# Weight layout of three out projections, place of the q blocks, and the last down projection's last chunk by token halves, in a three-layer block kernel on one core

## The chip, the cores and the metric

The kernel is one program for one core of a Trainium2 chip. The metric is device time in microseconds (us). Engines: TensorE (PE; PEld is its weight load), VectorE (DVE), ScalarE (ACT), GpSimd (POOL) and SyncE (SP), which issues most DMAs. Each engine runs its own instructions in program order and waits on semaphores for the others.

## The reference, cut to what matters

512 tokens of 1024 channels pass through three layers, all in float32; the third layer's output is normalised.

```python
# layer 1: gated delta rule                  # layer 2: stick-breaking attention
h = h + gdn_mixer(rms_norm(h), ...)          # ends in o @ gdn_w_out      (1024 x 1024)
h = h + swiglu(rms_norm(h), w_gu, w_down)    # 1024 -> 2 x 2816 -> 1024
h = h + sb_mixer(rms_norm(h), k, v, w_q)     # q = rms_norm(hn @ w_q) per head; ends in o @ sb_w_out
h = h + swiglu(rms_norm(h), w_gu, w_down)
# layer 3: latent attention and window attention, gated and added
x = h + mixed @ w_out_2                      # 1024 x 1024
x = x + conv_ffn(rms_norm(x), w_up, conv_w, conv_b, w_down)
out = rms_norm_2(x, final_norm_g)
```

In the stick-breaking mixer each head has scores z, softplus(z), a sum of it over later keys, weights exp(...) and values.

## The kernel before, in words

Everything is kept transposed: 128 channels on the partitions, 512 tokens along the free axis. `hT` holds the residual in 8 chunks (c), `ps` is the PSUM with 8 banks of 512. A product keeps float32 precision with three matmuls (`three`, L1745 to L1749): weights high times input high, weights high times input low, weights low times input high. The inputs' high and low parts are `xh` and `xl`, in 8 chunks (kc). One *block* is such a triple for one 128 x 128 piece of weights.

All weights come as one stream of units of 16 blocks (1 MB) in the order of use. SP loads unit u into `raw` (slot u % 2) once unit u-2 is split. ScalarE makes the high part `wh` (`split_hi`, L343, instruction L351), and VectorE then the low part `wl` (`split_lo`, instruction L933). Both wait for the count `units_used`, that is until TensorE has done unit u-2, for `wh` and `wl` have two slots too. TensorE waits for both parts (`unit_ready`). `hi_half` (L509) and `lo_half` (L1160) do the same in two instructions of 1024 columns.

An out projection (gdn_out, sb_out, mix_out) has 4 units. Output chunks 0 to 3 are accumulated in banks 0 to 3 input chunk by input chunk, since the mixer delivers input chunks one at a time; chunks 4 to 7 follow one after the other. In the stream the weights lie by output chunk: unit 0 has c 0 and 1, unit 1 has c 2 and 3, unit 2 c 4 and 5, unit 3 c 6 and 7 (`out_block`, L1840). Some blocks of c 0 to 3 are placed between other work of the mixers (`early_out` L2058, `OUT_AT`; steps 5 to 8 of the second mixer; steps 12 to 15 of the third and after them). `out_rest` (L1846) does what is left: kc 6 and 7 (7 in gdn_out) for c 0 to 3, then c 4 to 7. VectorE adds each finished chunk to `hT` and splits units 2 and 3 on the way (`split_out`, L974).

In the first mixer's last head, VectorE multiplies the normed values with their gain (`scale_out`, L1199, instruction L1201) and with silu(z) (`om_gdn`, L1291); ScalarE's copy (L384) and VectorE's `out_low` (L1206) then make input chunk 7.

The second mixer runs in steps t = 0 to 9 (TensorE's loop L2254 to L2280, ScalarE's `step` L731, VectorE's `step` L1371). On TensorE a step has the values of head t-2 (`head_values`, L2247), the scores of head t (L2209), the sum of squares of q of head t+1 (`q_sums`, L2196), the mask (L2219), the sums over later keys of head t-1 (`rest`, L2232 to L2236), and then filler: the dense block row of q of head t+3 (`q_dense`, 8 blocks, t = 0 to 4), or blocks of sb_out (3, 1, 1 and 19 in t = 5 to 8). On ScalarE a step has the square of q (`q_squares`, L690), the copy of the head's output (`head_out`, L729), copies of it into `xh` (L384), a unit's split, Ln and Exp for q's norm (L696, L698), Abs, Exp and Ln of softplus (L707, L709, L711), the Exp of head t-1's weights (L723) and softplus's high part (L717). On VectorE: `q_in` (L1341), a unit's split, `q_scale` (L1349), `remainder` (L1369), and softplus's three instructions (L1355, L1359, L1361), of which the last is its low part.

The end: the last feed-forward's down projection does 8 output chunks of 22 blocks. For the last, VectorE adds it to `hT` (L1045), ScalarE squares it (L918), TensorE adds that to the sum of squares over channels (`sum_norm_last`, L1765; fp32, two records for one matmul), ScalarE makes rstd by a table load, Ln and Exp (`make_rstd`, L367: L355, L371, L373), VectorE multiplies 8 chunks with gain and rstd (L1593), and SP sends each chunk out.

## Time and profile before

| | us |
|---|---|
| time, median of 3 runs | 2275.66 (2273.36 to 2275.94) |
| the profiled execution's own time | 2275.48 |
| its span, first to last instruction | 2273.4 |
| TensorE, matmuls | 2217.7 (98%) |
| VectorE, ScalarE, GpSimd busy | 1115.1, 923.8, 288.6 |

The span is that of one profiled execution; 2.1 us of its time lie outside it. The page gives busy time and groups of instructions; the waits name who released an engine; the windows give busy time and the granted clock of a stretch (1.00 is 2.4 GHz, 0.50 is 1.2 GHz); the timeline gives single instructions. Matmuls are pipelined: a record of 0.39 us starts 0.23 us after the one before it.

### The profile page before, as it was taken

Reading aid. Unit: us, or ns where it says so; the run is one execution under the profiler, and the core shown is the slowest. Engines: PE = TensorE matmul, PEld = TensorE weight load, DVE = VectorE, ACT = ScalarE, POOL = GpSimd, SP = SyncE. Lnnn points to the kernel's source line nnn. Section 1 sums busy time; section 2 is a strip of 40 time slices with the busy share of each in tenths; the row PEclk is TensorE's granted clock in tenths of the full one; section 3 lists DMA queues with packets and bytes.
Section 4 is the critical chain, followed back from the end, with each engine's and each line's share of the span. In section 5 each row is a group of like instructions: output and inputs, shape, how many; then the busy total and the mean of one; then the engine's idle time right before and its main releaser. Section 6 shows DMA issues by size and latency. Waiting matters only on the chain.

```text
span 2273.4 us, 28231 instructions
## 1 busy us (share of the span) xinstructions
PE 2217.7 (98%) x10980; PEld 1810.6 (80%) x10980; DVE 1115.1 (49%) x1413; ACT 923.8 (41%) x1243; POOL 288.6 (13%) x247
## 2 busy tenths in 40 slices
PE   7999999899999999998999999999999999999998
PEld 4788888688888888876888888888788777888886
DVE  5566656354443233464444432355665655555522
ACT  4544555232322234574332222255565554444311
POOL 0111112210000110001300001200000034222211
PEclk9999999999999999999999999999999999999999
DMA  3311111122222222210322222331111223222321
GB/s 134 112 56 38 47 47 38 56 93 92 92 93 105 98 86 82 77 37 17 111 92 92 96 107 93 120 109 68 67 54 56 70 69 117 92 92 94 107 95 56
DMA packets 30604, 185.37 MB, mean 82 GB/s; under 512 B 3104, under 2 KB 5536, under 8 KB 10160
## 3 DMA queue, kind: packets, MB, share of 16 engines
q1 hardware_dynamic: 28496, 176.46, 22.0%
q0 software_dynamic: 2016, 7.60, 1.0%
q8 instruction: 67, 1.10, 0.2%
q14 instruction: 25, 0.20, 0.0%
HBM read 179.83 MB, written 7.37 MB: 82 GB/s over the span
## 4 chain that ended last, share of the span: by engine, by line
PE 93%; DVE 3%; ACT 2%; issue 1%; DMA 0%; SPq 0%; POOL 0%; DVEq 0%; ACTq 0%; POOLq 0%
PE ps L1747 25%; PE ps L1749 25%; PE ps L1748 25%; PE ps L1955 4%; PE ps L2429 1%; PE ps L2372 1%; PE ps L2412 1%; PE ps L2247 1%; PE ps L2209 1%; PE ps L2439 1%; PE ps L1976 1%; DVE wl L933 0%; PE ps L1912 0%; PE ps L2370 0%; PE ps L2009 0%
## 5 line engine op out<-in xcount | busy, mean ns | idle before, releaser
L1747 PE MATMUL ps<-xh,wh 128*128 128x512 f32 x1888 | 766.1, 406 | 13.4 <-DVE wl L933 10.0
L1749 PE MATMUL ps<-xh,wl 128*128 128x512 f32 x1888 | 738.8, 391 | 0.0
L1748 PE MATMUL ps<-xl,wh 128*128 128x512 f32 x1888 | 737.4, 391 | 0.0
L351 ACT ACTIVATE wh<-raw 128x2048 fp32r<-128x2048 f32 x144 | 275.3, 1914 | 542.2 <-PE ps L1749 541.9
L933 DVE TENSOR_TENSOR wl<-raw,wh 128x2048 fp32r<-128x2048 f32 x144 | 336.6, 2337 | 310.0 <-ACT wh L351 310.0
L1747 PEld LDWEIGHTS ps<-xh,wh 128*128 128x128 f32 x1888 | 356.2, 189 | 93.3 <-issue 14.1
L1749 PEld LDWEIGHTS ps<-xh,wl 128*128 128x128 f32 x1888 | 355.4, 188 | 76.9
L1748 PEld LDWEIGHTS ps<-xl,wh 128*128 128x128 f32 x1888 | 356.6, 189 | 71.0 <-issue 4.8
L1747 PE MATMUL ps<-hid_h,wh 128*128 128x512 f32 x528 | 208.0, 394 | 0.0
L1749 PE MATMUL ps<-hid_h,wl 128*128 128x512 f32 x528 | 207.0, 392 | 0.0
L1748 PE MATMUL ps<-hid_l,wh 128*128 128x512 f32 x528 | 204.9, 388 | 0.0
L1011 DVE TENSOR_TENSOR scaled<-ps,rstd 128x1024 f32<-128x1024 f32 x44 | 53.9, 1225 | 192.9 <-PE ps L1749 192.9
L1749 PEld LDWEIGHTS ps<-hid_h,wl 128*128 128x128 f32 x528 | 99.1, 188 | 23.2
L1748 PEld LDWEIGHTS ps<-hid_l,wh 128*128 128x128 f32 x528 | 99.1, 188 | 22.2
L1747 PEld LDWEIGHTS ps<-hid_h,wh 128*128 128x128 f32 x528 | 99.3, 188 | 19.7
L1611 POOL TENSOR_TENSOR sq<-hT 128x512 f32<-128x512 f32 x41 | 48.2, 1177 | 289.9 <-DVE hT L1045 257.7
L1606 POOL TENSOR_TENSOR ssq<-hT 128x512 f32<-128x512 f32 x6 | 6.2, 1040 | 562.9 <-DVE hT L1045 507.0
L424 ACT ACTIVATE hid_h<-gu 128x512 f32 (+1 forms) x44 | 27.8, 632 | 110.2 <-DVE gu L1021 110.2
L1011 DVE TENSOR_TENSOR gu<-ps,rstd 128x1024 f32<-128x1024 f32 x22 | 26.9, 1225 | 85.8 <-PE ps L1749 85.8
L1613 POOL TENSOR_TENSOR ssq<-ssq,sq 128x512 f32<-128x512 f32 x41 | 61.4, 1498 | 3.2
L831 ACT ACTIVATE prob<-ps,nmax 128x512 f32<-128x512 f32 x32 | 22.0, 687 | 89.5 <-DVE nmax L1498 89.3
L1088 DVE SCALAR_TENSOR_TENSOR convd<-ps,vec,convd 128x511 f32<-128x511 f32 (+2 forms) x72 | 53.8, 747 | 2.0
(357 smaller groups left out, 2841.4 us busy)
## 6 DMA issues: line engine op xcount, KB each, us to landing
raw<-in_stream SPq DMA_DIRECT2D x159, 1024.0 KB, 4.8
hankd<-tabd SPq DMA_DIRECT2D x1, 3072.0 KB, 16.8
hank<-hankd POOLq DMA_DIRECT2D x4, 768.0 KB, 4.9
hT<-in_xT SPq DMA_DIRECT2D x4, 512.0 KB, 5.5
keepd<-hT POOLq DMA_DIRECT2D x1, 2048.0 KB, 9.9
hT<-keepd POOLq DMA_DIRECT2D x8, 256.0 KB, 4.6
out<-hT SPq DMA_DIRECT2D x8, 256.0 KB, 2.2
raw<-in_stream SPq DMA_DIRECT2D x2, 512.0 KB, 8.1
```

The source lines that it names most:

```text
L351: act.activation(wh[:, s, :], raw[:, s, :], ACT.Copy).then_inc(hi_made, 1)
L424: act.activation(hid_h[:, 2 * it + j, :], prod, ACT.Copy).then_inc(hid_hi_made, 1)
L933: dve.tensor_tensor(wl[:, s, :], raw[:, s, :], wh[:, s, :].bitcast(F32), ALU.subtract).then_inc(lo_made, 1)
L1011: dve.tensor_tensor(to[:, :, :], ps[:, b:b + 2, :], rstd[:, :].unsqueeze(1).to_broadcast([P, 2, SEQ]), ALU.mult).then_inc(gu_made, 1)
L1088: dve.scalar_tensor_tensor(convd[:, i, d:SEQ], ps[:, b, 0:SEQ - d], w, convd[:, i, d:SEQ], ALU.mult, ALU.add).then_inc(conv_step, 1)
L1611: pool.tensor_tensor(sq[:, :], hT[:, c, :], hT[:, c, :], ALU.mult).then_inc(squared, 1)
L1613: pool.tensor_tensor(ssq[:, :], ssq[:, :], sq[:, :], ALU.add).then_inc(summed, 1)
L1747: pe.matmul(out, w_hi, a_hi, start=start, stop=False)
L1748: pe.matmul(out, w_hi, a_lo, start=False, stop=False)
L1749: return pe.matmul(out, w_lo, a_hi, start=False, stop=stop)
L1955: m = pe.matmul(ps[:, b, cs(c)], left[:, c, :], right[:, c, :], start=True, stop=True)
L1976: m = pe.transpose(ps[:, (4, 4, 6)[k], cs(c)], T[:, c, :], mat("ident"))
```

## The change

- Stream layout (`by_half_then_chunk`): in the three out projections unit 0 has input chunks 0 to 3 of c 0 to 3, and unit 1 has chunks 4 to 7 of them. Units 2 and 3 are as before. `units_used` is counted at block (3,3) for unit 0; `half_done` counts c 0, 1, 2, 4 and 6.
- Unit 2 of each is split earlier: in gdn_out by halves among the last head's state work, in sb_out between steps 8 and 9 on ScalarE and before the low part of chunk 7 on VectorE, in mix_out before `fill_mixed(7)` on ScalarE and after the low part of chunk 7 on VectorE.
- Second mixer: the q blocks go by `Q_DENSE_AT` (head 4 by halves in steps 1 and 2, heads 5, 6, 7 in steps 3, 4, 5), `q_in` and `q_squares` by `Q_IN_AT`; the sb_out blocks are 4, 2 and 18 in steps 6 to 8; the splits of the units follow.
- Last down chunk: two passes over the 22 blocks with 256 tokens each, in banks 5 and 3; add, square, sum, Ln and Exp by halves; the gain is multiplied in by ScalarE ahead of it, rstd by VectorE over 4 chunks x 256 tokens; 8 output DMAs of 2 chunks x 256 tokens.

```diff
-HALF = {"gdn_out": 0, "sb_out": 4, "mix_out": 8}
+HALF = {"gdn_out": 0, "sb_out": 5, "mix_out": 10}
+Q_IN_AT = {2: 0, 3: 1, 4: 3, 5: 4, 6: 5, 7: 6}
+Q_DENSE_AT = {0: (3, 0, 8), 1: (4, 0, 4), 2: (4, 4, 8), 3: (5, 0, 8), 4: (6, 0, 8), 5: (7, 0, 8)}
...
-            for c in range(KC):
-                sp.wait_ge(final_made, c + 1)
-                sp.dma_start(io["out"][c * P:(c + 1) * P, :], hT[:, c, :]).then_inc(out_written, 16)
+            for k in range(8):
+                cs, tok = slice(2 * (k % 4), 2 * (k % 4) + 2), slice(256 * (k // 4), 256 * (k // 4) + 256)
+                sp.wait_ge(final_made, k // 2 + 1)
+                sp.dma_start(out_t[:, cs, tok], hT[:, cs, tok]).then_inc(out_written, 16)
...
             for c in range(TT):
                 values_out(HEADS - 1, c, 4)
+                if c >= 2:
+                    hi_half(U0["gdn_out"] + 2, c - 2)
             out_squares(HEADS - 1, 5)
...
             def step(t):
-                if t == 5:
-                    act.wait_ge(units_used, LAST_READER["sb_out"])
-                    for c in range(3):
-                        fill_chunk(om_sb, c, om_sb_made, 0)
-                q_squares(t + 2)
-                head_out(t - 2)
-                if t >= 5:
+                for h in Q_IN_AT:
+                    if Q_IN_AT[h] == t:
+                        q_squares(h)
+                head_out(t - 2)
+                if t == 6:
+                    act.wait_ge(units_used, LAST_READER["sb_out"])
+                    for c in range(4):
+                        fill_chunk(om_sb, c, om_sb_made, 0)
+                if t >= 6:
                     fill_chunk(om_sb, t - 2, om_sb_made, 0)
-                if t % 2 and t <= 5:
-                    split_hi(u0 + 2 + (t + 1) // 2)
+                if t in (1, 4, 6):
+                    split_hi(u0 + 3 + (1, 4, 6).index(t))
                 q_rstds(t + 1)
                 softplus(t)
                 weights(t - 1)
...
             for t in range(HEADS + 2):
+                if t == HEADS + 1:
+                    split_hi(U0["sb_out"] + 2)
                 step(t)
...
             fill_mixed(6)
+            split_hi(U0["mix_out"] + 2)
             fill_mixed(7)
...
-            act.activation(sq[:, :], hT[:, KC - 1, :], ACT.Square).then_inc(last_squared, 1)
-            make_rstd(6)
+            for c in range(KC - 1):
+                act.wait_ge(summed, 8 * (STATS["final"] - 1) + c + 1)
+                act.activation(hT[:, c, :], hT[:, c, :], ACT.Copy, scale=v("final_norm", c)).then_inc(gained, 1)
+            for a in range(2):
+                tok = slice(256 * a, 256 * a + 256)
+                act.wait_ge(resid_added, 8 * RESID["ffn2"] + KC + a)
+                act.activation(sq[:, tok], hT[:, KC - 1, tok], ACT.Square).then_inc(last_squared, 1)
...
+                act.activation(hT[:, KC - 1, tok], hT[:, KC - 1, tok], ACT.Copy, scale=v("final_norm", KC - 1)).then_inc(gained, 1)
+                act.wait_ge(norm_sum, 7 + a)
+                act.activation(sq[:, tok], ps[:, 6 + a, tok], ACT.Ln, bias=v("eps"), scale=1.0 / D_MODEL).then_inc(ln_made, 1)
...
+                act.activation(rstd[:, tok], sq[:, tok], ACT.Exp, scale=-0.5).then_inc(rstd_made, 1)
...
-                    if c in (3, 4, 6):
-                        split_lo(u0 + 2 + (3, 4, 6).index(c))
+                    if c in (4, 6):
+                        split_lo(u0 + 3 + (4, 6).index(c))
...
+            def finish():
+                for a in range(2):
+                    tok = slice(256 * a, 256 * a + 256)
+                    dve.wait_ge(*((chunk_done, 22) if a == 0 else (units_used, N_UNITS)))
+                    dve.tensor_tensor(hT[:, KC - 1, tok], hT[:, KC - 1, tok], ps[:, 5 - 2 * a, tok], ALU.add).then_inc(resid_added, 1)
+                    dve.wait_ge(rstd_made, 7 + a)
+                    dve.wait_ge(gained, KC + a)
+                    for q in range(2):
+                        h4 = hT[:, 4 * q:4 * q + 4, tok]
+                        dve.tensor_tensor(h4, h4, rstd[:, tok].unsqueeze(1).to_broadcast([P, 4, 256]), ALU.mult).then_inc(final_made, 1)
...
             for c in range(TT - 1):
                 state(HEADS - 1, c, 4)
+            lo_half(U0["gdn_out"] + 2, 0)
             scale_out(HEADS - 1, 5)
+            lo_half(U0["gdn_out"] + 2, 1)
             dve.wait_ge(o_scaled, HEADS)
...
             def step(t):
-                q_in(t + 2)
-                if t % 2 and t <= 5:
-                    split_lo(u0 + 2 + (t + 1) // 2)
+                for h in Q_IN_AT:
+                    if Q_IN_AT[h] == t:
+                        q_in(h)
+                if t in (1, 4):
+                    split_lo(u0 + 3 + (1, 4).index(t))
                 q_scale(t + 1)
+                if t == 6:
+                    split_lo(u0 + 5)
                 remainder(t - 1)
                 softplus(t)
...
             for c in (6, 7):
+                if c == 7:
+                    split_lo(U0["sb_out"] + 2)
...
+            split_lo(U0["mix_out"] + 2)
             split_out("mix_out", "ffn2", "norm2_2")
...
-            dve.wait_ge(rstd_made, 7)
-            for c in range(KC):
-                dve.scalar_tensor_tensor(hT[:, c, :], hT[:, c, :], v("final_norm", c), rstd[:, :], ALU.mult, ALU.mult).then_inc(final_made, 1)
...
+            def last_chunk(a):
+                tok = slice(256 * a, 256 * a + 256)
...
+                for fc in range(FC):
...
+                    m = three(ps[:, 5 - 2 * a, tok], wh[:, s, w], wl[:, s, w], hid_h[:, fc, tok], hid_l[:, fc, tok], fc == 0, fc == FC - 1)
...
+                    if a and fc == 6:
+                        sum_norm_last(0)
...
-                u, b = U0[name] + c // 2, KC * (c % 2) + kc
+                u, b = (U0[name] + kc // 4, 4 * (kc % 4) + c) if c < 4 else (U0[name] + c // 2, KC * (c % 2) + kc)
...
+                if (c, kc) == (3, 3):
+                    m.then_inc(units_used, 1)
...
-                q_dense(t + 3)
-                if t == 5:
+                if t in Q_DENSE_AT:
+                    q_dense(*Q_DENSE_AT[t])
+                if t == 6:
                     unit_ready(U0["sb_out"])
                     pe.wait_ge(q_copied, HEADS)
-                    for kc in range(3):
+                    for kc in range(4):
                         x_chunk_ready("sb_out", kc)
                         out_block("sb_out", 0, kc)
-                elif t == 6:
-                    x_chunk_ready("sb_out", 3)
-                    out_block("sb_out", 0, 3)
                 elif t == 7:
-                    x_chunk_ready("sb_out", 4)
-                    out_block("sb_out", 0, 4)
+                    unit_ready(U0["sb_out"] + 1)
+                    for kc in (4, 5):
+                        x_chunk_ready("sb_out", kc)
+                        out_block("sb_out", 0, kc)
...
-            sum_norm_last(6)
+            last_chunk(0)
+            last_chunk(1)
+            sum_norm_last(1)
```

## Rows read from the trace of the kernel before

**Rows 1.** The page: busy engines, and the two splits of a unit.

```profile
PE 2217.7 (98%) x10980; PEld 1810.6 (80%) x10980; DVE 1115.1 (49%) x1413; ACT 923.8 (41%) x1243; POOL 288.6 (13%) x247
...
L351 ACT ACTIVATE wh<-raw 128x2048 fp32r<-128x2048 f32 x144 | 275.3, 1914 | 542.2 <-PE ps L1749 541.9
L933 DVE TENSOR_TENSOR wl<-raw,wh 128x2048 fp32r<-128x2048 f32 x144 | 336.6, 2337 | 310.0 <-ACT wh L351 310.0
```

**Rows 2.** TensorE's waits, whole span: who released it, us in total, times, longest.

```profile
PE ps L1747 <- DVE wl L933: 10.0, 3, 3.4
PE ps L2247 <- ACT la L723: 5.8, 3, 2.5
```

**Rows 3.** Windows: length, busy time (count) of each engine, PEclk, DMA share, GB/s.

```profile
446.40:449.80 3.40, 3.40 (x10) 2.63 (x9) 1.91 (x1) 0.00 (x0) 3.32 (x2) 0.50 0.97 311
1036.90:1054.00 17.10, 14.96 (x59) 10.76 (x60) 8.89 (x7) 10.05 (x10) 1.28 (x1) 0.80 0.01 1
...
1878.10:1881.50 3.40, 3.40 (x15) 2.80 (x16) 3.10 (x2) 0.00 (x0) 3.26 (x2) 1.00 0.66 226
```

**Rows 4.** Timeline, gdn_out and mix_out: start, us, instruction, count, [idle before <-releaser].

```profile
432.67 0.60 ACT L543 ACTIVATE on<-ps 128x512 f32<-128x512 f32 x1 [0.87 <-PE ps L2029]
...
438.04 0.69 DVE L1206 TENSOR_TENSOR xl<-om_gdn,xh 128x512 fp32r<-128x512 f32 x1 [0.70 <-ACT xh L384]
...
438.88 0.47 PE L1747 MATMUL ps<-xh,wh 128*128 128x512 f32 x1 [1.67 <-DVE xl L1206]
...
1869.51 0.69 DVE L1586 TENSOR_TENSOR xl<-hT,xh 128x512 fp32r<-128x512 f32 x1 [1.92 <-ACT xh L864]
...
1878.05 0.47 PE L1747 MATMUL ps<-xh,wh 128*128 128x512 f32 x1 [3.38 <-DVE wl L933]
```

**Rows 5.** Timeline, second mixer: steps 4 and 5, and the start of step 8.

```profile
998.91 2.32 PE L2247 MATMUL ps<-la,v_tok 128*128 128x512 f32 x8
...
1001.27 0.60 ACT L729 ACTIVATE om_sb<-ps 128x512 f32<-128x512 f32 x1
...
1005.77 1.22 ACT L707 ACTIVATE soft<-ps 128x1280 f32<-128x1280 f32 x1
...
1007.37 0.44 PE L1747 MATMUL ps<-xh,wh 128*128 128x512 f32 x1
1007.57 1.49 DVE L1369 TENSOR_TENSOR la<-la,ps 128x1280 f32<-128x1280 f32 x1 [0.92 <-PE ps L2236]
...
1009.51 1.26 ACT L723 ACTIVATE la<-la 128x1280 f32<-128x1280 f32 x1
...
1012.57 1.48 DVE L1361 TENSOR_TENSOR soft_l<-soft,soft_h 128x1280 fp32r<-128x1280 f32 x1
1013.11 1.67 ACT L384 ACTIVATE xh<-om_sb 128x512 fp32r<-128x512 f32 x3 [0.67 <-PE ps L1749]
...
1049.26 3.38 PE L2247 MATMUL ps<-la,v_tok 128*128 128x512 f32 x8 [2.14 <-ACT la L723]
```

**Rows 6.** Windows with matmuls of 256 columns, then of 512; columns as in rows 3.

```profile
885.00:897.00 12.00, 12.00 (x100) 11.85 (x99) 3.69 (x3) 6.44 (x8) 0.00 (x0) 1.00 0.25 89
2210.00:2230.00 20.00, 20.00 (x89) 16.39 (x88) 3.62 (x3) 3.54 (x2) 2.35 (x2) 1.00 0.31 105
```

**Rows 7.** Timeline, the end of the kernel.

```profile
2261.27 0.69 DVE L1045 TENSOR_TENSOR hT<-hT,ps 128x512 f32<-128x512 f32 x1 [14.42 <-PE ps L1749]
...
2262.64 1.28 ACT L355 ACT_TABLE_LOAD   x1
2262.68 1.13 PE L1769 MATMUL ps<-sq,mats 128*128 128x512 f32 x2 [0.58 <-ACT sq L918]
...
2263.94 0.69 ACT L371 ACTIVATE sq<-ps,vec 128x512 f32<-128x512 f32 x1
2264.66 0.63 ACT L373 ACTIVATE rstd<-sq 128x512 f32<-128x512 f32 x1
2265.32 5.39 DVE L1593 SCALAR_TENSOR_TENSOR hT<-hT,vec,rstd 128x512 f32<-128x512 f32 x8 [3.36 <-ACT rstd L373]
```

More of the change, by code:

```diff
@@ L289, in build @@
         part_done, turned_done, a_made = sem("part_done"), sem("turned_done"), sem("a_made")
+        gained = sem("gained")
         x_in = [q_gs_made, exact_made, lat_rstd, kr_made]
@@ L634, in _ @@
             out_fill(7)
-            for u in range(U0["gdn_out"] + 2, U0["gdn_out"] + 5):
+            for u in range(U0["gdn_out"] + 3, U0["gdn_out"] + 5):
                 split_hi(u)
@@ L752, in _ @@
             for t in range(HEADS + 2):
+                if t == HEADS + 1:
+                    split_hi(U0["sb_out"] + 2)
                 step(t)
-            for u in range(U0["sb_out"] + 2, U0["sb_out"] + 5):
+            for u in range(U0["sb_out"] + 3, U0["sb_out"] + 5):
                 split_hi(u)
@@ L909, in _ @@
             fill_mixed(6)
+            split_hi(U0["mix_out"] + 2)
             fill_mixed(7)
-            for u in range(U0["mix_out"] + 2, U0["mix_out"] + 5):
+            for u in range(U0["mix_out"] + 3, U0["mix_out"] + 5):
                 split_hi(u)
@@ L1040, in ffn @@
                     for c in added_in(i):
+                        if conv and c == KC - 1:
+                            finish()
+                            continue
                         if c < KC - 1:
@@ L1820, in ffn @@
                     gate_up(3, it)
-                for b in range(KC * FC):
+                for b in range((KC - 1 if conv else KC) * FC):
                     c, fc = b // FC, b % FC
@@ L2058, in early_out @@
             def early_out(c, kc):
+                if c == 0 and kc % 4 == 0:
+                    unit_ready(U0["gdn_out"] + kc // 4)
                 if kc == 0:
-                    if c % 2 == 0:
-                        unit_ready(U0["gdn_out"] + c // 2)
                     if c == 0:
@@ L2176, in q_dense @@
                     pe.wait_ge(v_made, 4)
-                else:
+                elif k0 == 0:
                     pe.wait_ge(q_copied, 1 if h == 2 else h)
                 s, bank = (u0 + h // 2) % 2, 5 if h == 1 else 0
-                for kc in range(KC):
+                for kc in range(k0, k1):
                     if h == 0:
@@ L2459, in step @@
                         kc, c = n // 2, n % 2
-                        if n == 0:
-                            unit_ready(U0["mix_out"])
+                        if n % 8 == 0:
+                            unit_ready(U0["mix_out"] + n // 8)
                         if kc == 0:
@@ L2476, in _ @@
             values(ALL_STEPS - 3)
-            unit_ready(U0["mix_out"] + 1)
             pe.wait_ge(nm_made, 24 * PAIRS)
@@ L2515, in by_chunk, with by_half_then_chunk @@
     return w.reshape(k // P, P, n // P, P).transpose(2, 0, 1, 3)
+def by_half_then_chunk(w):
+    c = by_chunk(w)
+    first = c[0:4].transpose(1, 0, 2, 3).reshape(2, KC // 2 * 4, P, P)
+    return np.concatenate([first.reshape(-1, P, P), c[4:].reshape(-1, P, P)])
 def columns(v):
@@ L2541, in weight_stream @@
         add(c[[h, 8 + h, 16 + h, 24 + h]])
-    add(by_chunk(w["gdn_w_out"][0]))
+    add(by_half_then_chunk(w["gdn_w_out"][0]))
     def ffn(gu, down):
@@ L2555, in weight_stream @@
     add(by_chunk(w["sb_w_q"][0]))
-    add(by_chunk(w["sb_w_out"][0]))
+    add(by_half_then_chunk(w["sb_w_out"][0]))
     ffn(w["ffn_w_gu"][1], w["ffn_w_down"][1])
@@ L2578, in weight_stream @@
         add(np.stack([ga[a], gb[a], ga[b], gb[b]]))
-    add(by_chunk(w["w_out_2"][0]))
+    add(by_half_then_chunk(w["w_out_2"][0]))
     ffn(w["w_up_2"][0], w["w_down_2"][0])
```

51 lines of the change are left out of this document (34 added, 17 removed).

## The prediction, made before the changed kernel was timed

> **What bounds the kernel now.** I read the page first: TensorE has work for 2217.7 of 2273.4 us [rows 1]. So only two things can move the time: the 55.7 us in which TensorE has none, and stretches in which its matmuls run at less than full clock. Next the waits of TensorE by releaser: 10.0 us in three waits go to the low half of a weight unit (wl), 5.8 us in three to the stick-breaking weights (la, the Exp on ScalarE) [rows 2]. Third, the same stretches by windows: the granted clock is 0.50, so 1.2 GHz instead of 2.4, for 3.4 us behind the stall of the first out projection (and as long behind that of the second, a row like it), and its mean is 0.80 over the 17.1 us that hold two of the la stalls, which is two such drops; behind the third out projection's stall it is 1.00 [rows 3]. Each drop costs half of 3.4, 1.7 us. Last the end: after the last down matmul it takes 12.1 us (2261.27 to 2273.4) until the output is out [rows 7].
>
> **Out projections by halves of input chunks.** Before, unit 0 of a projection holds columns c 0 and 1, so it is in use until input chunk 7 comes; unit 2 can't be split until then. A split is 1.91 us on ScalarE and then 2.34 us on VectorE [rows 1], and the rest of chunk 7 covers only 1.4 of it. Hence about 3.3 us, three times. After, unit 0 holds chunks 0 to 3 of c 0 to 3 and is free after block (3,3). What is left for TensorE then is 12 blocks in the first and third projection and 14 in the second, at three matmuls of 0.227 each (88 weight loads in 20 us [rows 6]): 8.2 to 9.5 us, over 4.3 us of split. Unit 3 is free when it was before, and 16 blocks (10.9 us) of unit 2 cover it. The three stalls go. What is late next, projection by projection:
>
> First (gdn_out). Chunk 7 is already waited for: TensorE idles 1.67 us until its low part lands, which ends at 438.73 [rows 4]. The change puts two things into that chain. On ScalarE a half split stands ahead of the output squares, where only 0.87 us are idle [rows 4]; half of 1.91 is 0.96, plus gaps: 0.2 late. On VectorE the second half of the low split (half of 2.34: 1.2 us) stands between scale_out and the om_gdn product, and everything up to the low part of chunk 7 hangs on that product: 1.2 late. The cost is between 0 (if ScalarE's part is late enough to hide it, which no row suggests) and 1.4; I take 1.4. Saved: 3.3 - 1.4 = 1.9. The stall left, near 3 us, is as long as those followed by a drop, so I count the drop at 1.7 as staying.
>
> Second (sb_out). Head 7's values come after 18 blocks, as before after 19; the new split of unit 2 on both engines falls into time in which they have nothing [rows 5]. Saved: 3.3, and the drop of 1.7 behind it: 5.0.
>
> Third (mix_out). The low part of chunk 7 ends at 1870.2 (1869.51 + 0.69); the low split of unit 2 is queued behind it and needs 2.3 us, and TensorE has matmuls of chunks 6 and 7 till 1874.7 (1878.05 less the wait of 3.38) [rows 4]. Saved: 3.4, no drop there to win. Unit 1 is now wanted in step 14 instead of after step 15; it is split in steps 12 and 13, before that. Nothing.
>
> **The q blocks.** A step of the second mixer begins with head_values; 8.46 us later TensorE reaches its filler blocks (998.91 to 1007.37) [rows 5]. ScalarE's Exp of the weights, for which the next step waits, ends 11.86 after the step's start (1009.51 + 1.26) [rows 5]. So a step lasts the longer of 11.9 and 8.46 + 0.685 per block: 8 blocks give 13.9 and no wait, 4 give 11.2 and a wait of 0.7. Before, the short steps were 5 to 7 (3, 1, 1 blocks): 5.8 of waits and two drops, 9.2. After, the blocks by step are 8, 4, 4, 8, 8, 8, 4, 2, 18. New waits: 0.7 in each of steps 1 and 2. In step 3, q_in(4) stands behind the low part of soft, which ends 15.1 after the former step's start [rows 5], that is 3.2 into a step that follows one of 11.9; the square follows, and head_out is queued behind the square: q_sums waits 0.6 more (one ScalarE copy, 0.60 [rows 5]). Step 6 is the dear one. Its four copies of xh and the split of unit 1 stand on ScalarE behind head_out, which ends 2.95 after the start [rows 5]; five copies (0.56 each, three in 1.67) and 1.91 reach 7.7, Ln and Exp of q take 1.3 (0.69 and 0.63 on as many columns [rows 7]; 9.0), and from Abs to the end of the weights' Exp it is 5.0 [rows 5]: 14.0. On VectorE q_scale (0.7, as the 512 columns of [rows 4]) waits for that Exp, split_lo (2.3) for nothing more, and remainder (1.49 [rows 5]) is queued behind both: 13.5, so the weights end at 14.8 against TensorE's 11.2. Wait: 3.6, and a drop, 1.7. Step 7 has 2 blocks for 1: of its wait of 2.1 [rows 5] 1.4 stay. In step 8 rest(7) waits for soft's low part, which the slow clock hid before: 0 to 1.5, taken 1.0. Together 0.7 + 0.7 + 0.6 + 3.6 + 1.7 + 1.4 + 1.0 = 9.7, against 9.2: 0.5 lost. So the waits move rather than go.
>
> **The tail.** Two halves of 256 columns: 132 matmuls at 0.12 (99 weight loads in 12.0 us [rows 6]) are 15.8, against 66 at 0.227, 15.0: 0.8 more. The Trainium skill (TensorE: Matmul & The Clock Gate, Back-to-back issue gap) gives 262 cycles for 256 columns and 518 for 512, which at 2.4 GHz would make that 0.2 more; the rows say 0.12 and not 0.109, and they are used. The first half's sums stand inside the second half: two of 256 columns, at most one of 512 (1.13 with its drain [rows 7]), taken 0.9. The first half's add, square, Ln, Exp and two products (some 6 us) lie beside the second half's 7.9 us. After the last matmul, before: add 0.69, square 0.6, sum 1.13 beside a table load of 1.28, Ln 0.69, Exp 0.63, eight products in 5.39, and 2.7 till the end [rows 7]: 12.1 with gaps. After, on 256 columns, each between half and the whole of its row: add 0.45, square 0.40, sum 0.7, Ln 0.47, Exp 0.42, no table load, two products of 1024 columns at 1.2 (half of a 2048-column split), gaps 0.2: 5.0. The last two output DMAs, 512 KB together, start at once instead of 256 KB: 2.7 to 3.5, taken 3.1. 8.1 in all; 12.1 - 8.1 - 0.8 - 0.9 = 2.3 saved (1.0 to 3.8). The gain products on ScalarE lie before the last chunk is done.
>
> **Sum.** 1.9 + 5.0 + 3.4 - 0.5 + 2.3 = 12.1 us. The profiled execution took 2275.5 (span 2273.4 and 2.1 around it), the median is 2275.7: 2275.5 - 12.1 = 2263.4.
>
> **Rivals.** (A) The waits of the q steps and of chunk 7 don't come back: the refilled steps are covered and the drops go with them. For it: every step of 8 blocks shows no wait. Against: the order on ScalarE and VectorE is fixed. Then 3.3 + 1.7, 5.0, 3.4, 9.2 and 2.3 make 24.9: 2250.6. (B) The clock takes more back: two more drops, behind the waits of steps 2 and 7, 3.4, and the output's DMAs set the end, so that the tail gives nothing: 12.1 - 5.7 = 6.4, 2269.1. For it: drops stand behind stalls of 2.1 to 3.3, and one of 3.4 has none [rows 3], so which stall gets one isn't decided by its length alone. (C) The change doesn't do what it says: the splits of unit 2 still come after chunk 7, since the earlier release is followed by an engine that is not there yet. Then only tail and q steps stay, with 1.4 lost in the first: 2275.5 - 2.3 + 0.5 + 1.4 = 2275.1. Against: the release is one count at block (3,3), and in the order of both engines the new splits stand ahead of the adds, where the old ones stood behind three of them. (D) Slower: the short waits in consecutive steps hold the clock down. If steps 1 and 2, each with 11.2 us of matmuls, ran wholly at 1.2 GHz, and step 3's 14 as well, that adds 36.4 less 2.0 of waits that it covers: 2263.4 + 34.4 = 2297.8; it turns the sign from 12.1 us of added time, so 24 us of low clock. Against: behind the stalls of 2.1 and more the clock was back after 3.4 us [rows 3]. The Trainium skill (TensorE: Matmul & The Clock Gate, A second HAM failure mode) tells of short idle times between groups of matmuls throwing the clock back and forth; by that rule steps 1 to 3 would go this way, and no row here shows it.
>
> **How the numbers follow.** Forecast 0.66 (its own range 2260 to 2267: the drop in gdn_out gone or a second one come, and the tail's bounds), A 0.08, B 0.17, C 0.05, D 0.04. The forecast's neighbourhood and B are in the range, and half the way to A, since a drop less and a step better are likelier than all of A: 2257 to 2270. A measurement of this kernel can tell 0.2%, 4.6 us, from no change. Faster by more: 0.66 + 0.08 + 0.17 = 0.91; within: C, 0.05; slower: D, 0.04.
>
> **What the profile would show.** The wl waits at the three projections gone; a wait for xl before chunk 7 of gdn_out of about 3 us; la waits of about 0.7, 0.7, 3.6 and 1.4; two drops in place of the four behind these stalls; 8 us from the last matmul to the end. I am wrong if the la waits before steps 3 and 7 are absent (A's direction), if a wl wait stays (C), or if the clock row of the mixer's first steps shows 0.50 for longer than 3.4 us (D).

## The result, and the profile after

| | before | after |
|---|---|---|
| time, median (us) | 2273.92 (5 runs, 2272.76 to 2275.94) | 2260.7 (5 runs, 2260.11 to 2263.94) |
| ratio, 95% interval | | 0.9947 [0.9936, 0.9959] |
| span of the profiled execution | 2273.4 | 2258.0 |

The forecast was 2263.4, the range 2257 to 2270; the change was faster, as forecast, and clear of the interval. Of the 2.7 us by which the time was missed, 1.6 are the starting point: the forecast went from the profiled execution's 2275.5, and the median of the five runs beside the changed kernel is 2273.9.

The spans differ by 15.4 us, but 2.9 of it are there at 422.0 us (419.1 after), ahead of all that the change touches. That is start-up: the time until this instruction differs by up to 3.4 us over the thirteen profiles read here. The change has 12.5 in this pair of profiles; 12.1 was forecast. To split it I took instructions that both kernels have and compared the time between them:

| stretch | predicted saving | measured |
|---|---|---|
| gdn_out | 1.9 | 2.9 |
| second mixer and sb_out | 5.0 - 0.5 = 4.5 | 4.7 |
| mix_out | 3.4 | 3.7 |
| last down chunk and end | 2.3 | 1.3 |
| sum | 12.1 | 12.5, rounded apart |

TensorE's waits after, over the whole span (releaser, us in total, times, longest), which answer to [rows 2]:

```profile
PE ps L2318 <- ACT la L730: 6.4, 4, 3.9
PE ps L1794 <- DVE xl L1247: 2.9, 2, 2.7
PE ps L2280 <- DVE la L1402: 2.5, 1, 2.5
```

No wait for wl is left. The xl wait is the one before chunk 7 of gdn_out, 1.67 us before [rows 4], and the la waits of the first line are the second mixer's, four instead of three. The third line stands in both kernels and is not touched. Now the windows (length, busy time and count of PE, PEld, DVE, ACT, POOL, then the granted clock, DMA share, GB/s), which answer to [rows 3]:

```profile
436.40:439.80 3.40, 2.81 (x7) 2.26 (x8) 1.14 (x2) 0.00 (x0) 0.38 (x1) 0.50 0.75 294
1033.70:1037.10 3.40, 3.40 (x9) 2.10 (x8) 2.37 (x2) 0.75 (x1) 0.00 (x0) 0.50 0.32 130
951.80:955.20 3.40, 3.40 (x8) 1.92 (x8) 1.63 (x2) 1.73 (x2) 0.00 (x0) 0.50 0.00 0
```

The first is the drop to 1.2 GHz at chunk 7 of gdn_out, the second the one behind the new la wait of 3.9. The third is in both kernels, behind the untouched wait of 2.5. So two drops stand in place of the four behind the waits that the change moves, as forecast.

gdn_out after, ScalarE's, VectorE's and TensorE's instructions (start, us, instruction, count, idle time before and its releaser):

```profile
428.81 1.05 ACT L520 ACTIVATE wh<-raw 128x1024 fp32r<-128x1024 f32 x1
429.78 0.60 ACT L548 ACTIVATE on<-ps 128x512 f32<-128x512 f32 x1
...
433.64 1.22 DVE L1205 TENSOR_TENSOR wl<-raw,wh 128x1024 fp32r<-128x1024 f32 x1
434.78 0.68 DVE L1334 TENSOR_TENSOR om_gdn<-on,qkvz 128x512 f32<-128x512 f32 x1
...
436.15 0.69 DVE L1247 TENSOR_TENSOR xl<-om_gdn,xh 128x512 fp32r<-128x512 f32 x1 [0.69 <-ACT xh L389]
...
436.99 0.77 PE L1794 MATMUL ps<-xh,wh 128*128 128x512 f32 x1 [2.69 <-DVE xl L1247]
```

ScalarE's half split ends as its successor starts, and that successor is as early as before against the common instructions: it cost nothing. VectorE's half stands in the path and cost 1.0: the wait grew from 1.67 to 2.69. The clock fell 0.6 us before the wait ended (436.4 to 436.99), and so took about 1.4 of matmul time, not 1.7.

Step 6 of the second mixer after, the chain behind the wait of 3.9:

```profile
1020.09 0.60 ACT L736 ACTIVATE om_sb<-ps 128x512 f32<-128x512 f32 x1
1020.58 2.70 ACT L389 ACTIVATE xh<-om_sb 128x512 fp32r<-128x512 f32 x5
1023.18 1.90 ACT L356 ACTIVATE wh<-raw 128x2048 fp32r<-128x2048 f32 x1
1024.98 0.67 ACT L703 ACTIVATE qk_ln<-ps,vec 128x512 f32<-128x512 f32 x1
1025.68 0.63 ACT L705 ACTIVATE qk_ln<-qk_ln 128x512 f32<-128x512 f32 x1
...
1026.35 1.79 DVE L1392 SCALAR_TENSOR_TENSOR q_sb<-qk_raw,q_gs,qk_ln 128x512 f32<-128x512 f32 x1 [6.87 <-ACT qk_ln L705]
1028.06 2.28 DVE L954 TENSOR_TENSOR wl<-raw,wh 128x2048 fp32r<-128x2048 f32 x1
1030.26 1.48 DVE L1412 TENSOR_TENSOR la<-la,ps 128x1280 f32<-128x1280 f32 x1
...
1031.78 1.27 ACT L730 ACTIVATE la<-la 128x1280 f32<-128x1280 f32 x1 [1.72 <-DVE la L1412]
```

This is the order that the prediction wrote down: five copies and a split on ScalarE, then Ln and Exp, then q_scale, split and remainder on VectorE, then the Exp for which TensorE waits. Five copies took 2.7 instead of 2.8, but q_scale took 1.8 us instead of the 0.7 that was put down for it. What differs is what runs beside it. GpSimd makes the low parts of the five copies meanwhile:

```profile
1021.28 6.31 POOL L1668 TENSOR_TENSOR xl<-om_sb,xh 128x512 fp32r<-128x512 f32 x5 [193.53 <-ACT xh L389]
```

The last of the five runs from 1026.30 to 1027.59, and q_scale (1026.35) ends 0.55 us after it. It is so in all ten profiles in which a good part of q_scale lies beside such a subtraction: q_scale ends 0.54 to 0.56 after the subtraction does, and takes 1.8 us, or 0.84 to 0.87 where only 0.3 us lie beside it. With nothing beside it, it takes 0.75. So VectorE's instruction got on only when GpSimd's had ended; that GpSimd is the cause is read from the times, as no run moves its work alone.

The end after, which answers to [rows 7]:

```profile
2248.49 0.42 DVE L1031 TENSOR_TENSOR hT<-hT,ps 128x256 f32<-128x256 f32 x1 [1.98 <-PE ps L1796]
2248.94 0.42 ACT L934 ACTIVATE sq<-hT 128x256 f32<-128x256 f32 x1 [4.83 <-DVE hT L1031]
...
2249.41 0.70 PE L1817 MATMUL ps<-sq,mats 128*128 128x256 f32 x2 [0.53 <-ACT sq L934]
...
2250.15 0.47 ACT L938 ACTIVATE sq<-ps,vec 128x256 f32<-128x256 f32 x1 [0.25 <-PE ps L1817]
2250.65 0.42 ACT L940 ACTIVATE rstd<-sq 128x256 f32<-128x256 f32 x1
...
2251.10 2.36 DVE L1036 TENSOR_TENSOR hT<-hT,rstd 128x1024 f32<-128x1024 f32 x2 [2.19 <-ACT rstd L940]
```

The chain from the last add to the end of the last product is 2248.49 to 2253.46, 4.97 us; 5.0 was predicted. But the kernel ends at 2258.0, 4.5 behind it, where 3.1 was taken. The last chunk's two passes, from chunk 6's add to the last add, took 1.3 more than before (16.4 for 15.1; 1.7 predicted).

### The profile page after: what moved, and what is told of

The parts are those of the page before. It is cut to its first block, busy times and chain, and to the rows that moved or that the text cites. A ratio compares the mean times of both kernels' runs of the same rounds, so it can differ in the third digit from the quotient of the medians.

```text
span 2258.0 us, 28381 instructions
## 1 busy us (share of the span) xinstructions
PE 2211.8 (98%) x11050; PEld 1811.5 (80%) x11050; DVE 1113.1 (49%) x1411; ACT 928.7 (41%) x1255; POOL 286.7 (13%) x247
## 4 chain that ended last, share of the span: by engine, by line
PE 93%; DVE 3%; ACT 2%; issue 1%; DMA 0%; SPq 0%; POOL 0%; DVEq 0%; POOLq 0%
PE ps L1794 25%; PE ps L1796 25%; PE ps L1795 25%; PE ps L2025 4%; PE ps L2497 1%; PE ps L2440 1%; PE ps L2480 1%; PE ps L2507 1%; PE ps L2280 1%; PE ps L2046 1%; PE ps L2318 1%; PE ps L1982 0%; PE ps L2438 0%; PE ps L2079 0%; PE ps L2099 0%
## 5 line engine op out<-in xcount | busy, mean ns | idle before, releaser
L954 DVE TENSOR_TENSOR wl<-raw,wh 128x2048 fp32r<-128x2048 f32 x143 | 331.1, 2316 | 315.7 <-ACT wh L356 315.7
L1794 PE MATMUL ps<-hid_h,wh 128*128 128x512 f32 (+1 forms) x550 | 211.9, 385 | 0.0
L1796 PE MATMUL ps<-hid_h,wl 128*128 128x512 f32 (+1 forms) x550 | 210.6, 383 | 0.0
L1795 PE MATMUL ps<-hid_l,wh 128*128 128x512 f32 (+1 forms) x550 | 208.7, 379 | 0.0
```

The lines of the kernel that those rows point to most:

```text
L954: dve.tensor_tensor(wl[:, s, :], raw[:, s, :], wh[:, s, :].bitcast(F32), ALU.subtract).then_inc(lo_made, 1)
L1794: pe.matmul(out, w_hi, a_hi, start=start, stop=False)
L1795: pe.matmul(out, w_hi, a_lo, start=False, stop=False)
L1796: return pe.matmul(out, w_lo, a_hi, start=False, stop=stop)
```

## The experiments

Thirteen kernels in all have profiles here: before, after, and eleven for the questions below. Base is the changed kernel where nothing else is said; the kernel before had medians of 2272.3, 2272.2, 2272.5 and 2274.1 beside the four groups of runs. The times of kernels from different groups are compared with care for that reason: where the intervals of two ratios overlap, the stretch between common instructions in the profiles decides. Outside what a kernel changes and apart from drops of the clock, such stretches agree within 0.3 us.

**What makes the three gains in the out projections: layout or place?** The splits of unit 2 go back to their old places, the new layout stays.

```diff
...
-            split_hi(U0["mix_out"] + 2)
...
-                    if c in (4, 6):
-                        split_lo(u0 + 3 + (4, 6).index(c))
+                    if c in (3, 4, 6):
+                        split_lo(u0 + 2 + (3, 4, 6).index(c))
```

> The changed kernel with the splits of each out projection's unit 2 back at their old places (ScalarE: behind input chunk 7's copy; VectorE: behind the add of output chunk 2), the weights laid out by halves of input chunks as changed. The question: does the layout alone take the stalls away, or the earlier places, which the layout only allows? Theory (both are needed): at the old place VectorE's split starts behind the add of output chunk 2, when TensorE has one block of 0.69 us left of chunks 0 to 3, so TensorE waits for wl again, 2.3 to 2.5 us in each of the three projections (a split of 2.3, add of 0.7, less one block), while the wait for xl before chunk 7 of gdn_out falls by 1.0: 7.2 - 1.0 = 6.2 us more than the changed kernel, 2266.9, and up to 3.4 more if drops of the clock stand behind two of them. Rival (the layout alone is enough, since unit 0's slot is free early): no wl wait, and 1.0 us less than the changed kernel, 2259.7.

2269.89 (10 runs), ratio 0.9983 [0.9974, 0.9993]: 9.2 us more than the changed kernel, by intervals that do not overlap.

```profile
PE ps L1784 <- DVE wl L949: 8.2, 3, 3.4
...
PE ps L1784 <- DVE xl L1242: 1.9, 2, 1.7
...
1868.66 0.69 DVE L1008 TENSOR_TENSOR hT<-hT,ps 128x512 f32<-128x512 f32 x1 [0.31 <-DMA hT<-keepd]
1869.27 2.88 DVE L949 TENSOR_TENSOR wl<-raw,wh 128x2048 fp32r<-128x2048 f32 x1
```

The waits for wl are back, 2.40, 2.40 and 3.38, two drops stand behind the last two, and the xl wait is 1.66. The sum 2.40 + 2.40 + 3.38 + 3.4 - 1.0 - 1.4 is 9.2, as the medians have it; by the profiles it is 9.7 from 419 us on. The rival (layout enough) is out by 10 us. The third wait came longer than expected, since the add ahead of the split waited 0.3 for the residual's way back and the split took 2.88 instead of 2.3, with an instruction of GpSimd beside it from 1868.96 to 1870.00. So most of the gain is the earlier places'. The layout alone gives a little: the waits were 3.31, 3.31 and 3.38 before and are 2.40, 2.40 and 3.38 with it.

**Do the q blocks gain anything?** The first layout of the q blocks, of the sb_out blocks and of the splits between them is put back.

```diff
-Q_IN_AT = {2: 0, 3: 1, 4: 3, 5: 4, 6: 5, 7: 6}
+Q_IN_AT = {2: 0, 3: 1, 4: 2, 5: 3, 6: 4, 7: 5}
...
-                if t in (1, 4, 6):
-                    split_hi(u0 + 3 + (1, 4, 6).index(t))
+                if t in (1, 3, 5):
+                    split_hi(u0 + 3 + (1, 3, 5).index(t))
```

> The changed kernel with the q blocks, the squares and inputs of q, and the fillers of steps 5 to 8 back in their old places (8 blocks of q in steps 0 to 4; 3, 1, 1 and 19 blocks of sb_out); layout, early splits and tail stay changed. Theory: moving them only moves the waits. Waits for la of 1.2, 2.5 and 2.1 with two drops come back (9.2 us) and 0.5 + 0.5 + 0.3 + 3.9 + 1.4 + 0.6 with one drop (8.9) go: 2261.0, which can't be told from the changed kernel's 2260.7. Rival: the q blocks in later steps brought a part of the 13 us; then this is slower than the changed kernel by 3 us or more, 2264 or above.

2260.87, 0.9952 [0.9935, 0.9968], against 2260.7: no difference. The la waits of before are back (1.15, 2.54, 2.13) and the new ones gone:

```profile
PE ps L2316 <- ACT la L730: 5.8, 3, 2.5
```

That part of the change moves waits, worth 0.2 us by the medians, which the interval can't tell from nothing. In the two profiles two differences of the clock cancel: in gdn_out this one is 1.6 us longer, where the low clock lasts 6.8 us and not 3.4, and in the second mixer 1.5 shorter, where the untouched wait of 2.5 has no drop behind it.

**What makes step 6's wait?** Three kernels: only VectorE's split behind softplus (step6_lo), only ScalarE's four copies first (step6_cp), and both with ScalarE's split at the end of the step too (step6_all). In the diff of step6_all the first part stands on ScalarE ahead of q_squares and head_out (the copies' old place goes), the next two move ScalarE's split to the end of its step, the last is VectorE's.

```diff
+                if t == 6:
+                    act.wait_ge(units_used, LAST_READER["sb_out"])
+                    for c in range(4):
+                        fill_chunk(om_sb, c, om_sb_made, 0)
...
-                if t in (1, 4, 6):
-                    split_hi(u0 + 3 + (1, 4, 6).index(t))
+                if t in (1, 4):
+                    split_hi(u0 + 3 + (1, 4).index(t))
...
                 weights(t - 1)
                 softplus_hi(t)
+                if t == 6:
+                    split_hi(u0 + 5)
...
                 q_scale(t + 1)
+                remainder(t - 1)
+                softplus(t)
                 if t == 6:
                     split_lo(u0 + 5)
-                remainder(t - 1)
-                softplus(t)
```

> The changed kernel with step 6 of the second mixer put in another order: ScalarE's four copies into xh stand ahead of the square of q and of head_out, and the split of unit 1 of sb_out stands at the end of the step on both engines (behind softplus's high part on ScalarE, behind its low part on VectorE). Theory: the wait of 3.93 us before step 7 is the queue on ScalarE and VectorE in step 6; then it falls to the 0.5 of the other steps of 4 blocks, its clock drop goes, and the kernel is 3.4 + 1.7 = 5.1 us faster than the changed one: 2255.6. Rival: 4 blocks are too few to cover a step whatever the order, and the wait turns up at head_out or at the scores of step 7: under 2 us gained, 2259 or more.

> The changed kernel with one edit in step 6 of the second mixer: VectorE's low split stands behind softplus's low part instead of ahead of remainder. ScalarE's order is unchanged. Theory (as the prediction had it, the weights wait for VectorE's remainder, which is queued behind the split, with ScalarE close behind): remainder starts behind q_scale, and the Exp of the weights is then held by ScalarE's own softplus instructions, which end at 1030.20 in the changed kernel's trace where that Exp began at 1031.91: the wait before step 7 falls from 3.93 to 2.2 us. Rival (the chain runs through ScalarE alone, its copies and split, and VectorE's split is covered): the wait stays at 3.9.

> The changed kernel with one edit in step 6 of the second mixer: on ScalarE the four copies of finished head outputs into xh stand first in the step, ahead of the square of q and of head_out; the split's place is unchanged on both engines. Theory (ScalarE's order of work sets when q_scale and then VectorE's split and remainder can start; the four copies, 2.1 us, are done in time that ScalarE has idle at the step's start): the wait before step 7 falls by 2.1 us, from 3.93 to about 1.8. Rival (VectorE's split alone makes the wait, and the copies are covered): it stays at 3.9.

The four la waits of each, in that order:

```profile
PE ps L2320 <- ACT la L730: 2.9, 4, 1.4
```

```profile
PE ps L2318 <- ACT la L730: 4.5, 4, 2.1
```

```profile
PE ps L2318 <- ACT la L730: 3.8, 4, 1.4
```

The wait before step 7 is 3.93 in the changed kernel and 0.47, 2.10 and 1.40 in these (2.2 and 1.8 expected of the last two); in all three the drop behind it is gone. step6_all took 2256.09, 0.9934 [0.9917, 0.995], 4.6 less by the medians, though the two intervals overlap; step6_lo took 2258.19 and step6_cp 2258.86, one run each. The profiles decide: from the untouched wait of 2.5 to the first wait of the third layer it is 569.5 us in the changed kernel, 564.4 in step6_all, 566.3 in step6_lo and 565.5 in step6_cp, so the gains are 5.1 (5.1 expected), 3.2 and 4.0.

Each edit alone shortens the wait, so both engines are in the one chain, and either rival (ScalarE alone, VectorE alone) falls. But step6_cp's 2.53 isn't the copies' own time: ScalarE comes to Ln 1.49 us earlier in the step (5.76 after its start, not 7.25), since the copies now push the square of q back by 0.5, and the other 1.04 is q_scale, which has next to no GpSimd instruction beside it and takes 0.75 us instead of 1.79:

```profile
1021.40 6.39 POOL L1668 TENSOR_TENSOR xl<-om_sb,xh 128x512 fp32r<-128x512 f32 x5 [190.88 <-ACT xh L389]
...
1027.62 0.75 DVE L1392 SCALAR_TENSOR_TENSOR q_sb<-qk_raw,q_gs,qk_ln 128x512 f32<-128x512 f32 x1 [5.38 <-ACT qk_ln L705]
```

With all three edits, remainder no longer waits in VectorE's queue. It starts when TensorE's sums are done:

```profile
1024.36 0.84 DVE L1394 SCALAR_TENSOR_TENSOR q_sb<-qk_raw,q_gs,qk_ln 128x512 f32<-128x512 f32 x1 [5.24 <-ACT qk_ln L705]
1026.04 1.49 DVE L1414 TENSOR_TENSOR la<-la,ps 128x1280 f32<-128x1280 f32 x1 [0.83 <-PE ps L2309]
```

**gdn_out: is it VectorE's half split?** Its second half goes behind the low part of chunk 7.

```diff
             scale_out(HEADS - 1, 5)
-            lo_half(U0["gdn_out"] + 2, 1)
...
             out_low(7)
+            lo_half(U0["gdn_out"] + 2, 1)
```

> The changed kernel with one instruction moved: in gdn_out the second half of unit 2's low split stands behind the low part of chunk 7 instead of ahead of the om_gdn product. Theory: that half (1.2 us on VectorE) is what lengthened TensorE's wait for chunk 7 from 1.67 to 2.69 us. Then the wait is 1.7 again, no clock drop follows it (none of the drops stood behind a wait of under 2 us), and the kernel is 1.0 plus 1.3 to 1.7 us faster than the changed one (2260.7): about 2258.2. Rival: the wait is set by ScalarE's half split ahead of the output squares; then the wait stays at 2.7 and the time at 2260.7.

2258.04, 0.9939 [0.9922, 0.9955], 2.7 less than the changed kernel by the medians, with intervals that overlap. In the profiles the stretch from 419 us to the end of the untouched wait of 2.5 is 530.1 us against 532.5, 2.3 less. The wait is 1.69 again and the drop is gone:

```profile
436.49 0.47 PE L1794 MATMUL ps<-xh,wh 128*128 128x512 f32 x1 [1.69 <-DVE xl L1247]
```

**The tail.** First the old tail under the rest of the change (one pass of 512 tokens, eight products, eight DMAs of one chunk).

```diff
...
-            last_chunk(0)
-            last_chunk(1)
-            sum_norm_last(1)
+            sum_norm_last(6)
```

> The changed kernel with the old end: last down chunk in one pass over 512 tokens, sum and rstd over all, eight products with gain and rstd, eight output DMAs by chunk. Theory from the two traces: between the add of chunk 6 and the end of the span 27.2 us were needed before and 25.8 after, so the token halves are worth 1.4 us and this takes 2262.1. My prediction had 2.3 (2263.0); the rival that the tail gives nothing has 2260.7.

2263.3, 0.9956 [0.994, 0.9973]. The intervals of the two ratios overlap, so the medians' 2.6 doesn't decide. The profiles do: from the wait of 1.47 in the third mixer to the end it is 418.2 us here (1844.7 to 2262.8) and 416.8 in the changed kernel (1841.2 to 2258.0). The tail is worth 1.3, as by the pair of before and after. It is a firm number: in the eight profiles with the changed mix_out and the same instructions in the tail (best_two_q, below, differs only in who issues two DMAs), this stretch is 416.83 to 416.86 us. The two spans differ by 4.8, of which 3.1 is start-up (422.2 against 419.1).

Then what the last 4.5 us are. These kernels start from *best1*, which holds the gdn_out edit and all of step 6's. *best_two_q* issues two of the second half's four output DMAs from ScalarE, *best_fine* does the second half's products in four instructions of 2 chunks, with a DMA behind each, and *best_pad* has two additions of 8 columns more on VectorE while it waits for the second half. The first part of the diff is best_fine's, the second best_pad's.

```diff
-                sp.wait_ge(final_made, k // 2 + 1)
+                sp.wait_ge(final_made, k // 2 + 1 if k < 4 else k - 1)
...
-                    for q in range(2):
-                        h4 = hT[:, 4 * q:4 * q + 4, tok]
+                    n = 4 - 2 * a
+                    for q in range(KC // n):
+                        h4 = hT[:, n * q:n * q + n, tok]
...
+                    if a == 1:
+                        for x in range(2):
+                            dve.tensor_tensor(scaled[:, 0, 8 * x:8 * x + 8], scaled[:, 1, 0:8], scaled[:, 1, 8:16], ALU.add)
```

> Two changes of order together, in place of one: in gdn_out VectorE's second half of unit 2's low split stands behind the low part of chunk 7, and in step 6 of the second mixer the four copies stand first on ScalarE, with both parts of the split of the sb_out unit moved to the end of the step. Theory (the two stalls are independent, each with its own drop of the clock): the savings of the two single kernels, 2.6 and 4.6 us by their medians against the changed kernel's 2260.7, add up: about 2253.5, ratio 0.991; the wait for xl before chunk 7 is 1.7, the la wait before step 7 is 0.5, and no drop stands behind either. Rival (what is taken away early is given back later, since a faster first mixer only moves the drops): no better than the better of the two, 2256.1.

> As best1, and of the second token half's four output DMAs the second and the fourth are issued by ScalarE instead of SyncE, so that no DMA stands behind another issue. Theory (rate): the issue is not what bounds the end, so counted from the end of the last product nothing changes, 4.4 us (at most 0.1 less). Rival (issue time: each DMA takes SyncE 0.45 us, one behind the other): the last DMA starts 0.41 us earlier, and the end comes as much earlier, 4.0 us.

> As best1, and in the second token half the product with rstd is done in four instructions of 2 chunks x 256 tokens instead of two of 4 chunks, with one output DMA behind each. It tells what sets the 4.4 us between the end of the last product and the end of the kernel, where 3.1 was predicted. Theory (rate: 1 MB in pieces of 1 KB goes out at 341 GB/s from the first DMA's first data on): the first DMA starts 0.6 us earlier, so the end comes 0.5 us earlier counted from the second half's Exp, though the last product ends 0.2 later. Rival (a fixed cost behind the last product: two issues of 0.45 and the latency of a DMA): the last DMA is now issued 0.4 earlier than before (one issue behind the last product, not two), against 0.2 of later product: 0.2 us or less. Second rival (more instructions on VectorE cost what they give): 0 or later.

> As best1 (both changes of order), and VectorE does two additions of 8 columns each on data that nobody reads any more, in the time in which it waits for the last down projection's second token half. The question: in best1 and in the changed kernel one DMA engine is still sending 1 KB pieces alone for 0.75 us when the other 15 have ended, and in both an 8 KB transfer of an instruction queue runs in the middle of the output's transfer; in best_fine, with two VectorE instructions more, that 8 KB transfer came before the output's data and all engines ended together. Theory (the instruction transfer delays its DMA engine, and its time hangs on how many instructions stand ahead of it): with two instructions more, at another place, it comes before the output's data again, the lone engine is gone, and the time from the end of the second half's Exp to the end of the kernel is 6.2 to 6.4 us instead of 6.9. Rival (the lone engine comes from the two products of 4 chunks or from the DMAs' pairs, which best_fine changed and this kernel does not): 6.9, whenever the 8 KB come.

| | time, ratio | first product to the end |
|---|---|---|
| best1 | 2253.7, 0.9919 [0.9906, 0.9933] | 6.9 (2243.4 to 2250.3) |
| best_two_q | 2253.36, 0.9913 [0.9899, 0.9927] | 6.9 (2244.4 to 2251.2) |
| best_pad | 2252.36, one run | 6.2 (2244.1 to 2250.3) |
| best_fine | 2252.01, 0.991 [0.9895, 0.9925] | 5.6 (2242.6 to 2248.2) |

best1 first: the two savings were to give 2253.5 together, and 2253.7 was measured. Its clock is at full speed from 24 us after the start until its matmuls end; the drop behind the untouched wait of 2.53 did not come either, which none of the edits aimed at.

Two issuing engines change nothing (the last DMA is issued 0.4 us earlier behind the last product, and the end stays), so issue time doesn't set the end. Now the DMA's view of the end, GB/s in 40 equal slices of a window of 6.3 us, from 2244.7 in best1, 2243.2 in best_fine and 2244.7 in best_pad, in that order:

```profile
GB/s 0 0 0 0 0 111 345 306 364 364 325 306 358 371 332 319 293 390 358 384 319 332 345 332 286 78 26 26 20 26 0 0 0 0 0 0 0 0 0 0
DMA packets 1089, 1.06 MB, mean 168 GB/s; under 512 B 64, under 2 KB 1088, under 8 KB 1088
...
q14 instruction: 1, 0.01, 0.3%
```

```profile
GB/s 0 0 0 0 0 0 124 351 345 306 384 325 332 312 377 351 332 299 351 390 332 319 364 351 325 332 59 0 0 0 0 0 0 0 0 0 0 0 0 0
```

```profile
GB/s 0 0 0 0 0 0 0 0 0 39 299 319 319 397 338 312 306 397 351 332 286 384 364 358 325 332 358 345 345 156 0 0 0 0 0 0 0 0 0 0
```

In all three 1 MB leaves in some 3.1 us at about 340 GB/s. In best1 there is a foot of 0.7 us at 26 GB/s: pieces one behind the other, each 46 ns. 1 KB in 46 ns is 22 GB/s, about a 16th of the 340, so it is one of the 16 DMA engines. There an instruction queue's transfer of 8 KB (q14) ran in the middle of the output; in the other two it came before the output's data, and the foot is gone. The changed kernel, best_two_q and the six others with this tail have both the transfer and the foot. best_pad doesn't touch products or DMAs and is 0.75 us shorter, against 0.5 to 0.7 expected; its time is a single run, but the eight profiles above agree within 0.03. The rival (the shape of products and DMAs makes the foot) falls. best_fine has 0.5 on top of that: its first DMA starts half a us sooner behind the first product, and the end comes as much sooner, though the last product ends 0.15 later. The medians of best_fine and best1 have overlapping intervals; from the wait of 1.47 to the end the profiles have 415.6, 416.1 (best_pad) and 416.9. So the end is set by when the transfer starts and its rate. That the 8 KB delay the very engine that lags is argued from the timing: the trace doesn't name the engine.

## Why the prediction was right, and where its terms were off

**Out projections.** Right: all three wl waits went, and what became late next was named, the xl wait in gdn_out alone. gdn_out: predicted 1.9, measured 2.9. The term "ScalarE 0.2 late, VectorE 1.2 late" was 0 and 1.0: ScalarE's half split fitted into its idle time, since its record of 1.05 overlaps those of its neighbours by some 0.1 at each side, which leaves 0.87, just what was idle [rows 4]; VectorE's half, 1.22 long, overlaps its neighbours likewise and costs 1.0. The drop was counted at 1.7 and took 1.4, because it began inside the wait. mix_out: 3.4 predicted, 3.7 measured. The recorded wait isn't all that a stall costs:

```profile
1874.29 0.39 PE L1749 MATMUL ps<-xh,wl 128*128 128x512 f32 x1
1878.05 0.47 PE L1747 MATMUL ps<-xh,wh 128*128 128x512 f32 x1 [3.38 <-DVE wl L933]
1878.36 0.40 PE L1748 MATMUL ps<-xl,wh 128*128 128x512 f32 x1
```

These are the matmuls around mix_out's wait in the kernel before. They start 3.76 and 0.31 us apart, where two running ones start 0.23 apart: 3.6 us lost for a recorded wait of 3.38. The same 0.2 is in gdn_out's 2.9, and brings layout_only's sum of 9.2 to the profiles' 9.7. Rival C is refuted by the missing wl waits.

**The q blocks.** Predicted waits 0.7, 0.7, 0.6, 3.6, 1.4, 1.0; measured 0.49, 0.50, 0.32, 3.93, 1.44, 0.60, with one drop behind the 3.93. With the drop that is 9.0, against 9.7 predicted and 9.2 before: "the waits move rather than go" holds, and step6_all, step6_lo and step6_cp show by which instructions. The forecast of 3.6 for step 6 is 0.3 from the measured 3.93 with one term much too small, q_scale's 0.7 for 1.79, which shorter terms on ScalarE made up in part (Exp of q ended 8.6 us into the step, not 9.0). The first of the waits hangs on a drop: where the untouched wait of 2.5 has none behind it, as in best1, it is 1.16 instead of 0.49. Rival A (they don't come back) is refuted: the la waits are there. Rival D too: steps 1 and 2 show waits of 0.5, and the clock was low there for 3.4 us, in the drop that before has as well, and at full speed for the rest up to 1033.7. So the rule of the Trainium skill that stood behind it (TensorE: Matmul & The Clock Gate, A second HAM failure mode) is not borne out here, at waits of 0.5 between 11 us of matmuls.

**The tail.** The mis-sized term is "2.7 to 3.5, taken 3.1" for the time behind the last product. It was 4.5. It took 256 KB to stand behind the last product before and 512 KB after, and both are too little, for the kernel before sends at its full rate already while its eight products run:

```profile
2267.00:2272.00 5.00, 0.00 (x0) 0.00 (x0) 3.71 (x6) 0.00 (x0) 0.00 (x0) 0.50 1.03 381
```

Its data run from 2266.95 to 2272.58, and when the last product ends (2270.71), 0.70 of the 2.10 MB are still to go. After, it is 1.00 of the second half's 1.05 MB. Bytes by rate fit both: 0.70 MB at 381 GB/s are 1.8 us, and with 0.8 from the last data to the end 2.7; 1.00 MB at 341 GB/s are 2.9, and with 0.75 for the lone engine and 0.9 behind the data 4.5. Without the lone engine, which no row of before shows, that sum would have said 3.8. The tail's other terms were 5.0 for 4.97 and 1.7 for 1.3, the sums' matmuls being short (0.59 for two of 256 columns, pipelined). Rival B had the output bound as one half of it; in direction that half came true, but the tail still gave 1.3.

**The sum.** That 12.1 came so near to 12.5 is in part luck: gdn_out was taken 1.0 too low and the tail 1.0 too high, and the two cancel.

**The drops.** "Which stall gets one isn't decided by its length alone" is borne out. The unchanged wait of 2.53 has a drop behind it in eight of the thirteen profiles and none in five (q_undone, best1, best_two_q, best_fine, best_pad). And the same wait of 3.38 in mix_out had none before [rows 3], and one in layout_only, the first window here; behind a wait of 2.40 there is none, the second, or one, the third:

```profile
1873.40:1876.80 3.40, 3.40 (x10) 2.63 (x9) 2.04 (x1) 0.00 (x0) 3.28 (x2) 0.51 0.87 311
441.50:444.90 3.40, 3.34 (x15) 2.80 (x16) 2.96 (x2) 0.00 (x0) 3.32 (x2) 1.00 0.63 200
1074.70:1078.10 3.40, 3.40 (x10) 2.62 (x9) 2.48 (x2) 0.00 (x0) 3.32 (x2) 0.51 0.85 272
```

That I counted one drop at gdn_out and one at step 6 came true, but by the same rows it could have been none or three: that term has an uncertainty of its own of some 3 us.

## What to carry to other kernels

Before work is moved into a stretch that has no wait, list what each engine has queued there and add it up to the instruction for which TensorE waits: here a split that nobody needed yet stood ahead of a remainder that everybody waited for, and another order of copies and split in that one step gave 5.1 us, where the whole placing of the q blocks gave nothing that could be measured. Look at GpSimd too: here a VectorE instruction of 0.75 us took 1.8 beside one of GpSimd's. An earlier release of a buffer gives little (1.8 of 10.0 us of waits here) until the work that uses it is moved ahead of what it was queued behind. At a kernel's end, sum the output's transfer as one piece, from the first product to the last byte at the measured rate, and let the first product be small so that the transfer starts early.

## What the runs showed that I had not expected

- The output in pieces of 1 KB went out at about 341 GB/s, 46 ns each, and in pieces of 2 KB before at about 381 GB/s, 86 ns each.
- An 8 KB instruction transfer amid the output goes with 0.75 us at the end in which one DMA engine sends alone; with two tiny instructions more on VectorE it came ahead of the output, and the time from the first product on fell from 6.9 to 6.2 us.
- VectorE's q_scale, 0.75 us alone, ended 0.55 us behind the GpSimd subtraction that ran beside it, whenever that was, and so took up to 1.79.
- The low clock came in stretches of 3.4 or of 6.8 us. In q_undone, behind the same wait of 2.69 that has 3.4 in the changed kernel:

```profile
436.70:443.50 6.80, 6.24 (x15) 4.92 (x16) 3.16 (x5) 0.69 (x1) 3.37 (x3) 0.50 0.36 142
```
